# Memory attention's value product turned round, and the first block's expert lists made ready apart from their gates

## The chip, the cores and the metric

One core of a Trainium2 chip runs one program. TensorE (PE) multiplies, VectorE (DVE), ScalarE (ACT) and GpSimd (POOL) work on vectors, SyncE (SP) issues most transfers; ACT and POOL issue some too. The metric is the device time of one execution in microseconds (us), the median of several runs; lower is better.

## The reference

One decoder layer on 320 tokens: 256 of a prompt and 8 sequences of 8. Branches (convolution, DeltaNet, attention into a memory) are gated, summed and projected; then comes PEER, in which each token picks 128 single-neuron experts. The two parts that the change touches:

```python
def memory_attention(q, mem_k, mem_v):          # 4 heads of 256, 256 memory tokens; the 8 sequences have their own k and v
    s = jnp.einsum('blhd,bmhd->bhlm', q, mem_k).astype(jnp.float32) * (XA_HEAD_DIM ** -0.5)
    p = jax.nn.softmax(s, axis=-1)
    o = jnp.einsum('bhlm,bmhd->blhd', p, mem_v)

def block(xblk):                                 # peer_ffn, 8 heads, 16 experts each
    t1, i1 = lax.top_k(s1, PEER_TOPK)            # s1, s2: scores of a head's query halves against 128 keys each
    t2, i2 = lax.top_k(s2, PEER_TOPK)
    top, pos = lax.top_k(cand, PEER_TOPK)        # cand: the 16 x 16 sums t1 + t2; cidx: i1 * 128 + i2
    eidx = jnp.take_along_axis(cidx, pos, axis=-1)
    gate = jax.nn.softmax(top, axis=-1)
    u = expert_u[eidx]                           # 128 rows of 2048 floats (1 MB) for each token
    act = jax.nn.gelu(jnp.einsum('td,thkd->thk', xblk, u))
    v = expert_v[eidx]                           # another 1 MB
    return jnp.einsum('thk,thkd->td', gate * act, v)
```

## The kernel before

Everything is float32 and feature-major (128 features on the partitions, tokens in the free dimension), but for the hidden rows of the expert stage. SP streams 1 MB weight tiles into slots 0 to 5 of `ring`, a tile being issued when the one four (later five) before it has been used (`tiles_done`). The stages, one after the other: memory keys and values, convolution, 16 DeltaNet heads, four attention heads (`att`, 1190 to 1362 us), the merge of the branches for the first block of 128 tokens (`merge0`), its output projection (`out0`) and its queries for the experts (`pq0`, 1720 to 1785 us). From then on the expert stage runs over 320 tokens, and beside its first 128 tokens the same merge, projection, queries and picking are done for the other 192 tokens (`second_block(s)`, a step s behind each token).

**Attention.** For a head `a`, PE multiplies the scores of the prompt (L729, all 256 tokens) and of the 8 sequences (L737). L737 puts four column groups of 32 side by side: the masked queries of two sequences are stationary, a sequence's 128x256 keys move. Then it projects the queries of head `a + 1` (L522), while DVE and ACT do the softmax (L1641 to L1648, L1114), transposes the probabilities (L746, L747), and makes the values. Here the stationary operand is 128x128 of values: for the prompt 4 products with 256 moving columns (L758), for the sequences 32 products with 8 moving columns (L764), each recorded as two. Values come as tiles 4 and 5 of a head, freed when their half of L764 is done. DVE copies the result into `xoT0` and `xoT1` (L1658).

**First block, hidden rows.** After the first query tile of `pq0`, PE turns the normed hidden rows to token-major (L792). ACT and DVE split them into three bfloat16 parts, 512 columns at a time, in turn (L1136, L1697, L1140, L1701), ACT stores them to `hparts`, and SP waits for the store (`parts_out`) ahead of `token_parts` (L467) and of the loads of `merge1`.

**First block, picking.** For each of 8 heads `topk_part` runs on DVE: parts 0 and 1 take 16 of 128 twice, part 2 takes 16 of the 256 sums, part 3 turns positions into expert numbers (for each of the two key halves: compare L1764, multiply L1768, sum L1770; then L1772) and makes the head's gate by softmax (L1752, ACT's Exp L1154, L1775 to L1779). A head's scores need two query tiles. ACT takes its orders in one list: it copies a query (L1166), a score (L1160), and does a head's Exp in between.

**The lists.** PE runs three merge tiles of the second block and only then turns both lists, `efull` (numbers) and `gfull` (gates) (L835, L836). DVE copies them to `eT` and `gT` (L1786, L1787), clears two banks, and `lists_ready` at 2 lets POOL begin its gathers (L1953 for u, L1956 for v): four slots each, 1 MB a gather, a slot refilled when `dotted` or `summed` says that its token was used. DVE's dot (L1851) is two instructions of 1.22 us per token.

```python
            pool.wait_ge(lists_ready, 2)
            with pool.Fori(0, 8) as i:
                gather_pair(i)
```

Of the kernel before, what the change touches and what calls it, by code (L numbers as in the profile page):

```python
# [21 lines left out]
P = 128  # L22
D = 2048
# [101 lines left out]
def build(nc, io):  # L125
    with ExitStack() as ctx:
# [126 lines left out]
        xqs = (xq, seven[:, 4 * P:4 * P + 2 * TOKENS].rearrange("p (t n) -> p t n", t=2))  # L253
        mx, sm, r3 = sb("mx", [P, UNITS]), sb("sm", [P, UNITS]), sb("r3", [P, UNITS])
# [17 lines left out]
        def topk_buffers(flat, at, units):  # L272

            def piece(*shape, dt=F32, words=None):
                f = view(flat, at, int(np.prod(shape)) if words is None else words)
                if dt != F32:
# [6 lines left out]
                        cand2=piece(units, TOPK * TOPK), eq=piece(n, TOPK, dt=BF16, words=n * TOPK // 2),  # L283
                        v16=piece(2, units, TOPK), iu=piece(2, units, TOPK, dt=U32), i16=piece(2, units, TOPK, dt=BF16, words=n),
                        fdig=piece(2, n, dt=BF16, words=n), pos=piece(units, TOPK, dt=U32), digits=piece(2, n, dt=U32),
                        e12=piece(2, n), top=piece(units, TOPK), gx=piece(units, TOPK), gsum=piece(units, 1),
# [7 lines left out]
        hres0 = mmf[:, 0:1024].rearrange("p (n d) -> p n d", n=2)  # L294
# [27 lines left out]

        def softened(s):

            if s < LAST_TOPK:
                return [(s - TOPK_AT) // 4] if s >= TOPK_AT and (s - TOPK_AT) % 4 == 2 else []
            return {LAST_TOPK + 1: [6], LAST_TOPK + 4: [7]}.get(s, [])
# [183 lines left out]
        def _(pe):  # L511
# [211 lines left out]
            for a in range(AH):  # L723
# [122 lines left out]
            def turn_pair(n):  # L846
# [3 lines left out]
                for x in two:  # L850
                    if n:
                        pe.wait_ge(rest_ready, 8 + 4 * (n - 1) + x + 1)
                    turn_hidden(ps[6 + x], P if t == 1 else NS, t * P, q + x).then_inc(turned, 1)

            def query_tile(m):
                arrived("pq1", m % 4, m // 4)
                if m == 0:
                    pe.wait_ge(rest_ready, 8 + 12 + 1)
                project(regions[0], m % 4, h1_, free=((q_read[(m - 1) % 2], 8 + (m - 1) // 2 + 1),))

            def scores1(m):
                b = m % 2
                pe.wait_ge(q_read[b], 8 + m // 2 + 1)
                if m == 0:
                    pe.wait_ge(rest_ready, 8 + 12 + 2)
# [21 lines left out]
            def turn_lists():  # L887
                pe.wait_ge(picked, 2 * PH)
                pe.wait_ge(turned_read, 8)
                for n, name in enumerate(("efull", "gfull")):  # L890
                    for t in two:
                        w = P if t == 0 else NS
                        last = nc.tensor.transpose(ps[6 + n][:, t * P:t * P + w], tk1[name][0:w, t, :], ident[0:w, 0:w])
                last.then_inc(lists_turned, 1)
# [64 lines left out]
        def _(act):  # L959
# [150 lines left out]
            for a in range(AH):  # L1110
# [7 lines left out]
                act.wait_ge(pt_done, a + 1)  # L1118
                fn(pT[:, :, 0:TP], ps[6].rearrange("p (m t) -> p m t", m=2), ACT.Copy).then_inc(pt_ready, 1)
            with act.Fori(0, KT) as i:  # L1120
# [10 lines left out]
            def split_pair(n, t, q, w, banks):  # L1131
# [5 lines left out]
                hres = hres1 if t else hres0  # L1137
                for x in two:
                    act.wait_ge(rest_ready, 4 * n + x + 1)
                    fn(p[1][0:w, (q + x) * 512:(q + x + 1) * 512], hres[0:w, x, :], ACT.Copy).then_inc(part_taken, 1)  # L1140

            def store_parts(n, t):
                act.wait_ge(rest_ready, 4 * n + 4)
                act.wait_ge(part_taken, 4 * n + 4)
# [6 lines left out]
            def soften(n):  # L1151
                gx = (tk0 if n < PH else tk1)["gx"]
# [9 lines left out]
            for m in range(KT):  # L1162
# [4 lines left out]
                if m == 0:  # L1167
                    for n in two:
# [890 lines left out]
```

## Time and profile before

| | |
|---|---|
| median of 3 runs (lowest, highest) | 3784.81 us (3783.73, 3788.24) |
| the profiled execution | 3782.26 us |
| its span in the trace | 3780.2 us |
| mean granted clock of TensorE | 0.835 |
| busy: PE, DVE, ACT, POOL | 84%, 47%, 17%, 21% |
| gathers (software queue) | 671.13 MB, from 1822.56 us on |

The trace gives each instruction its start and its length; an engine's idle time is given with what ended it. The granted clock is a share of full speed (1.0 is 2.4 GHz, 0.5 is 1.2 GHz); a stretch's figure is a mean over it. Lengths of matmuls are modelled, starts are recorded.

### The profile page before, as it was taken

The page shows a single profiled execution, that of the slowest core. Times are in us where ns is not written, and L with a number is a line of the kernel's source. Part 1 is how long each engine was busy: PE and PEld are TensorE (multiplying, and loading weights), DVE is VectorE, ACT ScalarE, POOL GpSimd, SP SyncE. Part 2 cuts the span into 40 slices and gives each one's busy share as a digit, 9 for nine tenths or more (in the row PEclk, how much of TensorE's full clock was granted, in tenths as well). Part 3 has the DMA queues.
Part 4 walks back from the last instruction along what each step waited for, and adds up shares of the span by engine and source line. Part 5 has one row for each costly group of instructions (what it writes and reads, how often), then busy time and mean ns, then how long its engine had stood idle before and what let it go on. Part 6 is the DMA issues. An engine that isn't in the chain of part 4 may idle for free.

```text
span 3780.2 us, 50527 instructions
## 1 busy us (share of the span) xinstructions
PE 3168.2 (84%) x17796; PEld 2135.5 (56%) x17796; DVE 1791.1 (47%) x4287; ACT 628.5 (17%) x1657; POOL 777.1 (21%) x889
## 2 busy tenths in 40 slices
PE   8999999999997999998899999878665666665554
PEld 7767777777775789998788888645310000000000
DVE  2396656666564200006433333359955444444544
ACT  1001222222222100001011101122211111111111
POOL 1000111121111000000222222232233333333332
PEclk9999999999998889999999999978755555555555
DMA  5433334333332468886899999999999999999997
GB/s 189 147 120 137 129 107 132 118 120 119 115 96 91 172 225 294 292 290 237 334 419 417 419 417 418 418 406 417 356 397 418 416 418 418 416 418 414 415 416 301
DMA packets 203479, 1096.07 MB, mean 290 GB/s; under 512 B 27360, under 2 KB 69216, under 8 KB 75952
## 3 DMA queue, kind: packets, MB, share of 16 engines
q0 software_dynamic: 92160, 671.13, 43.2%
q1 hardware_dynamic: 104096, 401.31, 29.8%
q10 hardware_dynamic: 7120, 22.22, 1.5%
q8 instruction: 68, 1.11, 0.1%
q14 instruction: 35, 0.29, 0.0%
HBM read 1062.88 MB, written 31.70 MB: 290 GB/s over the span
## 4 chain that ended last, share of the span: by engine, by line
PE 43%; DMA 29%; DVE 17%; issue 8%; ACT 2%; POOL 2%; DVEq 0%; SPq 0%; ACTq 0%; POOLq 0%
PE psum L522 24%; DMA branches<-in_peer_u,idx 23%; PE psum L588 8%; DMA ring<-in_peer_u,idx 5%; DVE branches L1851 2%; PE psum L946 2%; DVE branches L1385 2%; DVE ring L1851 2%; DVE branches L1488 2%; PE psum L651 1%; PE psum L660 1%; PE psum L657 1%; PE psum L764 1%; PE psum L349 1%; DVE rs L1582 1%
## 5 line engine op out<-in xcount | busy, mean ns | idle before, releaser
L1851 DVE CUSTOM_DVE_ANT_0 ring<-ring,psum 128x1024 f32<-128x1024 f32 x480 | 566.7, 1219 | 638.3 <-DMA ring<-in_peer_u,idx 577.6
L522 PE MATMUL psum<-hT,ring 128*128 128x128 f32 (+2 forms) x4800 | 803.8, 328 | 29.2 <-DMA ring<-in_w_glu 10.5
L522 PEld LDWEIGHTS psum<-hT,ring 128*128 128x128 f32 x4800 | 720.7, 196 | 104.9 <-issue 31.8
L929 PE MATMUL psum<-shared,selb 24*128 24x512 bf16 x1280 | 304.8, 524 | 453.4 <-DVE dots L1851 443.9
L929 PEld LDWEIGHTS psum<-shared,selb 24*128 24x128 bf16 x1280 | 56.6, 96 | 1022.4 <-DVE dots L1851 921.7
L588 PE MATMUL psum<-hT,ring 128*128 128x320 f32 x2112 | 621.9, 436 | 9.9 <-DMA ring<-in_w_att 7.7
L588 PEld LDWEIGHTS psum<-hT,ring 128*128 128x128 f32 x2112 | 383.0, 191 | 152.8 <-issue 20.3
L1245 ACT ACTIVATE ge<-dots 128x1 f32<-128x1 f32 x320 | 94.3, 295 | 1485.9 <-DVE dots L1851 1480.3
L1851 DVE CUSTOM_DVE_ANT_0 branches<-branches,psum 128x1024 f32<-128x1024 f32 x160 | 189.0, 1218 | 238.9 <-DMA branches<-in_peer_u,idx 220.8
L522 PE MATMUL psum<-branches,ring 128*128 128x128 f32 (+1 forms) x2048 | 295.5, 303 | 6.3 <-ACT shared L1181 6.3
L522 PEld LDWEIGHTS psum<-branches,ring 128*128 128x128 f32 x2048 | 285.9, 192 | 10.0 <-issue 10.0
L1953 POOL DMA_INDIRECT ring<-in_peer_u,idx x240 | 225.9, 941 | 287.1 <-DVE dots L1851 249.9
L522 PE MATMUL psum<-mm,ring 128*128 128x128 f32 (+2 forms) x1504 | 250.5, 328 | 1.2 <-DVE mm L1677 1.2
L522 PEld LDWEIGHTS psum<-mm,ring 128*128 128x128 f32 x1504 | 232.9, 192 | 17.5 <-issue 5.0
L1665 DVE SCALAR_TENSOR_TENSOR shared<-shared,psum 128x128 f32<-128x128 f32 (+1 forms) x96 | 27.9, 318 | 361.8 <-PE psum L522 361.8
L1933 POOL TENSOR_TENSOR mm<-mm,shared 128x256 f32<-128x256 f32 (+1 forms) x112 | 100.9, 934 | 255.1 <-DVE mm L1520 255.1
L946 PE MATMUL psum<-branches,wz 128*8 128x512 f32 x640 | 126.9, 879 | 15.5 <-ACT wz L1247 10.2
L1385 DVE SCALAR_TENSOR_TENSOR branches<-branches,dwp 128x256 f32<-128x256 f32 x464 | 138.0, 378 | 0.0
L1944 POOL COPY idx<-shared 128x8 uint32 x40 | 7.8, 195 | 621.5 <-DVE shared L1787 621.3
L946 PE MATMUL psum<-vmem,wz 128*8 128x512 f32 x640 | 129.5, 895 | 5.5 <-ACT wz L1247 3.0
L1956 POOL DMA_INDIRECT vmem<-in_peer_v,idx x80 | 75.1, 939 | 270.9 <-PE psum L946 259.2
L946 PE MATMUL psum<-mm,wz 128*8 128x512 f32 x640 | 126.7, 878 | 2.1
(393 smaller groups left out, 3101.6 us busy)
## 6 DMA issues: line engine op xcount, KB each, us to landing
ring<-in_w_merge SPq DMA_DIRECT2D x160, 1024.0 KB
ring<-in_w_head SPq DMA_DIRECT2D x64, 1024.0 KB
ring<-in_w_outp SPq DMA_DIRECT2D x32, 1024.0 KB
ring<-in_w_pq SPq DMA_DIRECT2D x32, 1024.0 KB
ring<-in_w_att SPq DMA_DIRECT2D x24, 1024.0 KB, 7.0
ring<-in_w_mem SPq DMA_DIRECT2D x16, 1024.0 KB
ring<-in_w_glu SPq DMA_DIRECT2D x16, 1024.0 KB
out_qkv_out<-ring ACTq DMA_DIRECT2D x16, 520.5 KB
```

Of the source, the lines that this page charges most:

```text
L349: last = nc.tensor.matmul(out, ones[:], src[:, kt, :], start=kt == 0, stop=kt == count - 1)
L522: last = mat(out, ring[:, j, (k0 + kt) * P:(k0 + kt + 1) * P], src[:, kt, :], start=kt == 0, stop=kt == kts - 1)
L588: last = mat(ps[j][:, 0:TOKENS], ring[:, j, kt * P:(kt + 1) * P], hT[:, kt, :], start=kt == 0, stop=kt == KT - 1)
L929: last = mat(ps[q][:, :], selb[32 * q:32 * q + 24, j, :], hb[32 * q:32 * q + 24, g_, :], start=True, stop=True)
L946: last = mat(psum[32 * q:32 * q + group, 4 + g_, :], wz[:, g_, r % group, :], v_slots[s][:, q * 512:(q + 1) * 512], start=r % group == 0, ...
L1245: fn(ge[:, g_, j:j + 1], dots[:, g_, j, 0:1], ACT.Gelu_apprx_tanh, bias=dots[:, g_, j, 1:2]).then_inc(ge_ready, 1)
L1385: st(v.scalar_tensor_tensor(acc_, src, w, acc_, ALU.mult, ALU.add))
L1488: st(v.reciprocal(nrm[:, :, :], nrm[:, :, :]))
L1851: v.tensor_tensor_reduce(out=u, in0=u, in1=x, scale=1.0, scalar=0.0, op0=ALU.mult, op1=ALU.add, accum_out=dots[:, g_, j, half_:half_ + 1]) ...
L1933: g.tensor_tensor(lt[:, l, 0:units * P].rearrange("p (u n) -> p u n", u=units), at3[:, 0:units, :], lm[:, l, :].unsqueeze(1).to_broadcast( ...
L1953: g.indirect_dma_start(u_slots[s], None, io["peer_u"], at_).then_inc(u_in[s], 16)
L1956: g.indirect_dma_start(v_slots[s], None, io["peer_v"], at_).then_inc(v_in[s], 16)
```

## The change

The sequences' value product has the probabilities stationary, in four column groups, and the values moving: 16 products of 128x32 with 128x256, as L737 has. Its result is token-major; ACT copies it to `otok`, and two products with a selection of `ident` turn it back. The prompt's products stand between. The first block's hidden rows are copied whole to `hres0`, ACT makes the three parts at query tiles 0, 4 and 8, and POOL makes the two rests. In both blocks the two key halves are picked in one set of instructions of twice the size, and the softmax is done once for all eight heads, behind the picking. The first block's numbers are turned after two merge tiles (twice; the first copy goes nowhere), the gates after the third; the gathers wait for the numbers alone.

PE in the attention, and behind `pq0`:

```diff
-                pe.wait_ge(pt_ready, 2 * a + 2)
+                pe.wait_ge(pt_ready, 3 * a + 2)
...
+                for m in two:
+                    for c in two:
+                        for q in range(4):
+                            b = 2 * q + c
+                            at_ = (b % 4) * 512 + m * 256
+                            last = mat(ps[3][32 * q:32 * q + 32, 0:256], pz[:, m, c, 32 * q:32 * q + 32],
+                                       ring[:, 4 + b // 4, at_:at_ + 256], start=m + c == 0, stop=m + c == 2, skip_group_check=True)
+                            if m + c == 2 and q % 2:
+                                last.then_inc(tiles_done, 1)
...
-                for b in range(NBATCH):
-                    c = slice(TP + b * TS, TP + (b + 1) * TS)
-                    for d in two:
-                        for m in two:
-                            at_ = (b % 4) * 512 + m * 256 + d * P
-                            last = mat(ps[4 + d][:, c], ring[:, 4 + b // 4, at_:at_ + P], pT[:, m, c], start=m == 0, stop=m == 1)
-                    if b % 4 == 3:
-                        last.then_inc(tiles_done, 1)
+                pe.wait_ge(pt_ready, 3 * a + 3)
+                for d in two:
+                    last = mat(ps[4 + d][:, TP:TOKENS], otok[:, d * P:(d + 1) * P], tokens_of_slots, start=True, stop=True)
+                last.then_inc(pt_done, 1)
...
-            for k in range(3):
+            for k in range(2):
                 merge_tile(0, k)
             pe.wait_ge(picked, PH)
-            nc.tensor.transpose(ps[0][:, 0:P], tk0["efull"][:, 0, :], ident[:]).then_inc(summed, SLOTS)
+            nc.tensor.transpose(ps[2][:, 0:P], tk0["efull"][:, 0, :], ident[:]).then_inc(summed, SLOTS - 1)
+            nc.tensor.transpose(ps[0][:, 0:P], tk0["efull"][:, 0, :], ident[:]).then_inc(lists_turned, 1)
+            merge_tile(0, 2)
+            pe.wait_ge(picked, PH + 1)
             nc.tensor.transpose(ps[1][:, 0:P], tk0["gfull"][:, 0, :], ident[:]).then_inc(lists_turned, 1)
+            nc.tensor.transpose(ps[2][:, P:2 * P], tk0["gfull"][:, 0, :], ident[:]).then_inc(summed, 1)
```

ACT in the attention, then its first parts in `pq0` (called at query tiles 0, 4 and 8):

```diff
+                act.wait_ge(tiles_done, min(FIRST["att"] + 6 * a + 8, FIRST["att"] + 6 * AH))
+                fn(otok, ps[3][:, 0:256], ACT.Copy).then_inc(pt_ready, 1)
...
+            def first_parts(m):
+
+                act.wait_ge(rest_ready, m)
+                if m == 0:
+                    for q in range(4):
+                        act.wait_ge(turned, q + 1)
+                        last = fn(hres0[:, q * 512:(q + 1) * 512], ps[q], ACT.Copy)
+                    last.then_inc(part_taken, 1)
+                    act.wait_ge(part_taken, 1)
+                fn(parts[:, m, :], hres0, ACT.Copy).then_inc(part_taken, 1)
+                if m == 2:
+                    act.wait_ge(part_taken, 4)
+                    act.dma_start(hparts[0:P], parts[:, :, :]).then_inc(parts_out, 16)
...
-            soften(6)
-            soften(7)
-            for n in range(3):
-                gate(0, n)
+            gate(0, 0)
+            gate(0, 1)
+            soften(0)
+            gate(0, 2)
...
-                for n in softened(s):
-                    soften(PH + n)
+                if s == LISTS_AT:
+                    soften(1)
```

DVE: part 3 of `topk_part` compares, multiplies and sums both halves at once (the compare is shown), and the softmax is outside:

```diff
+                    st(v.tensor_tensor(eq, fdig.rearrange("p x n -> p (x n)").unsqueeze(2).to_broadcast([P, 2 * units * TOPK, TOPK]),
+                                       iota16[:].unsqueeze(1).to_broadcast([P, 2 * units * TOPK, TOPK]), ALU.is_equal))
...
+            def gates_in(tk, n):
+
+                units = tk["units"]
+                for t in range(units):
+                    top = tk["gfull"][:, t, :].rearrange("p (h k) -> p h k", h=PH)
+                    gx = tk["cand"][:, t, 0:PH * TOPK].rearrange("p (h k) -> p h k", h=PH)
+                    last = v.tensor_tensor(gx, top, top[:, :, 0:1].to_broadcast([P, PH, TOPK]), ALU.subtract)
+                last.then_inc(soft_in, 1)
...
+            def gates_out(tk, n):
+                units = tk["units"]
+                dve.wait_ge(soft_out, n + 1)
...
+            gates_in(tk0, 0)
+            v.memset(ps[5], 0.0).then_inc(dotted[1], SLOTS)
             dve.wait_ge(lists_turned, 1)
             v.tensor_copy(eT[:, 0:N0], ps[0][:, 0:N0]).then_inc(lists_ready, 1)
+            gates_out(tk0, 0)
+            st(v.memset(ps[4], 0.0))
+            dve.wait_ge(lists_turned, 2)
             v.tensor_copy(gT[:, 0:N0], ps[1][:, 0:N0]).then_inc(lists_ready, 1)
...
+                elif s == LISTS_AT:
+                    gates_out(tk1, 1)
```

POOL, ahead of its gathers:

```diff
+            for m in two:
+                pool.wait_ge(part_taken, m + 2)
+                if m:
+                    pool.wait_ge(rest_ready, m)
+                g.tensor_tensor(hres0, hres0, parts[:, m, :], ALU.subtract).then_inc(rest_ready, 1)
...
             pool.wait_ge(stored, 32)
-            pool.wait_ge(lists_ready, 2)
+            pool.wait_ge(lists_ready, 1)
```

`gates_out` waits for ACT's one Exp over all heads, then sums, inverts and multiplies (L1775 to L1779 of before, over 128 elements), and adds one to `picked`.

## Rows read from the trace of the kernel before

**Rows 1.** Page, the span in 40 slices: what the DMA engines moved

```profile
GB/s 189 147 120 137 129 107 132 118 120 119 115 96 91 172 225 294 292 290 237 334 419 417 419 417 418 418 406 417 356 397 418 416 418 418 416 418 414 415 416 301
```

**Rows 2.** Windows: stretch, its us, busy us by engine, granted clock, DMA share, GB/s

```profile
1247.00:1265.00 18.00, 17.65 (x113) 14.74 (x113) 1.42 (x9) 0.29 (x1) 0.00 (x0) 0.72 0.50 176
1344.00:1362.00 18.00, 16.84 (x72) 16.03 (x71) 1.02 (x4) 0.00 (x0) 0.00 (x0) 0.50 0.22 75
1785.00:1811.00 26.00, 12.86 (x66) 12.40 (x66) 24.32 (x115) 0.87 (x4) 0.00 (x0) 0.85 0.45 162
2700.00:2755.00 55.00, 28.15 (x132) 8.67 (x132) 51.43 (x172) 15.21 (x34) 14.78 (x17) 0.63 0.81 300
```

**Rows 3.** Groups by line, 1190 to 1362 us: busy us, mean ns, idle

```profile
L764 PE MATMUL psum<-ring 128*128 128x8 f32 x256 | 43.5, 314 | 0.0
...
L729 PE MATMUL psum<-kmem,ring 128*128 128x256 f32 x32 | 13.0, 579 | 0.0
...
L737 PE MATMUL psum<-ring 128*32 128x256 f32 x128 | 9.0, 430 | 0.0
```

**Rows 4.** Timeline of PE in the attention: start, us, what, count

```profile
1224.83 1.89 PE L729 MATMUL psum<-kmem,ring 128*128 128x256 f32 x8
...
1249.18 9.46 PE L764 MATMUL psum<-ring 128*128 128x8 f32 x64
...
1258.49 3.76 PE L729 MATMUL psum<-kmem,ring 128*128 128x256 f32 x8
...
1347.18 13.66 PE L764 MATMUL psum<-ring 128*128 128x8 f32 x64
```

**Rows 5.** The attention's tile loads, from issue to landing

```profile
DMA to landing us min/median/max: 4.9/7.0/7.5
```

**Rows 6.** Timeline of DVE, the first block's picking

```profile
1735.89 0.49 DVE L1720 MAX8 vmem<-vmem 128x8 f32<-128x128 f32 x2 [3.28 <-ACT vmem L1160]
...
1795.98 0.49 DVE L1720 MAX8 vmem<-vmem 128x8 f32<-128x128 f32 x2
...
1802.14 0.42 DVE L1764 TENSOR_TENSOR vmem<-vmem,iota 128x256 bf16<-128x256 bf16 x1
...
1804.62 0.18 DVE L1772 SCALAR_TENSOR_TENSOR vmem<-vmem 128x16 f32<-128x16 f32 x1
...
1805.32 0.49 DVE L1720 MAX8 vmem<-vmem 128x8 f32<-128x128 f32 x2
...
1820.02 0.29 DVE L1786 CAST shared<-psum 128x128 uint32<-128x128 f32 x1 [5.40 <-PE psum L836]
```

**Rows 7.** The chain that ended last, in order of time

```profile
1749.32 0.50 DVE vmem L1720 x2
```

**Rows 8.** Timeline of DVE, a head of the second block

```profile
2646.29 0.69 DVE L1764 TENSOR_TENSOR branches<-branches,iota 128x512 bf16<-128x512 bf16 x1
...
2648.22 0.75 DVE L1764 TENSOR_TENSOR branches<-branches,iota 128x512 bf16<-128x512 bf16 x1
```

**Rows 9.** Timeline of ACT during the first block's queries

```profile
1727.93 1.23 ACT L1140 ACTIVATE mm<-mm 128x512 bf16<-128x512 f32 x2 [0.27 <-DVE mm L1697]
...
1739.05 0.28 ACT L1166 ACTIVATE shared<-psum 128x128 f32<-128x128 f32 x1 [3.30 <-PE psum L522]
```

**Rows 10.** Timeline of PE: the third merge tile

```profile
1811.62 8.07 PE L522 MATMUL psum<-branches,ring 128*128 128x192 f32 x32 [6.34 <-ACT shared L1181]
```

**Rows 11.** Timeline of POOL: the first gather

```profile
1822.56 1.16 POOL L1953 DMA_INDIRECT ring<-in_peer_u,idx  x1 [1.53 <-DVE psum L1789]
```

**Rows 12.** Timeline of POOL in a DeltaNet head

```profile
734.53 6.31 POOL L1933 TENSOR_TENSOR mm<-mm,shared 128x384 f32<-128x384 f32 x7 [14.47 <-DVE mm L1520]
```

**Rows 13.** Timeline of DVE in the same head

```profile
733.30 0.56 DVE L1516 TENSOR_TENSOR ring<-ring 128x384 f32<-128x384 f32 x1
...
734.83 1.11 DVE L1522 TENSOR_TENSOR ring<-ring,shared 128x384 f32<-128x384 f32 x1
```

**Rows 14.** Timeline of SP's queue

```profile
1770.15 3.48 SPq L467 DMA_DIRECT2D shared<-hparts  x8
```

More of the change, by code:

```diff
@@ L253, in build @@
         xqs = (xq, seven[:, 4 * P:4 * P + 2 * TOKENS].rearrange("p (t n) -> p t n", t=2))
+        at = [4 * P + 2 * TOKENS]
+        pz = view(seven, at, 4 * P).rearrange("p (m c n) -> p m c n", m=2, c=2)
+        otok = view(seven, at, 2 * P)
+        tokens_of_slots = ident[:].rearrange("p (q n) -> p q n", q=4)[:, :, 0:2 * TS]
         mx, sm, r3 = sb("mx", [P, UNITS]), sb("sm", [P, UNITS]), sb("r3", [P, UNITS])
@@ L893, in turn_lists @@
                         last = nc.tensor.transpose(ps[6 + n][:, t * P:t * P + w], tk1[name][0:w, t, :], ident[0:w, 0:w])
[L894 removed]
+                    last.then_inc(lists_turned, 1)
             def second_block(s):
@@ L1166, in _ @@
                 fn(qs[:, b, 0:N0], ps[4 + b][:, 0:N0], ACT.Copy).then_inc(q_read[b], 1)
-                if m == 0:
-                    for n in two:
-                        split_pair(n, 0, 2 * n, N0, (2 * n, 2 * n + 1))
-                    store_parts(1, 0)
-                else:
+                if m:
                     take_scores0(m - 1)
-                if m >= 5 and m % 2:
-                    soften((m - 5) // 2)
+                if m in (0, 4, 8):
+                    first_parts(m // 4)
             take_scores0(KT - 1)
@@ L1648, in _ @@
                 v.tensor_tensor(pp, pp, sm[:].unsqueeze(2).to_broadcast([P, UNITS, MEM]), ALU.mult).then_inc(pn_ready, 1)
-                dve.wait_ge(pt_done, a + 1)
+                dve.wait_ge(pt_done, 2 * a + 1)
                 for m in two:
-                    last = v.tensor_copy(pT[:, m, TP:].rearrange("p (q n) -> p q n", q=4),
-                                         ps[7][:, m * P:(m + 1) * P].rearrange("p (q n) -> p q n", q=4)[:, :, 0:2 * TS])
+                    for c in two:
+                        at_ = slice(c * TS, (c + 1) * TS)
+                        last = v.tensor_copy(pz[:, m, c, :].rearrange("p (q n) -> p q n", q=4)[:, :, at_],
+                                             ps[7][:, m * P:(m + 1) * P].rearrange("p (q n) -> p q n", q=4)[:, :, at_])
                 last.then_inc(pt_ready, 1)
@@ L1710, in topk_part @@
                 combos = [(x, t) for x in two for t in range(units)]
-                v16, iu, sc2, cand, cand2, top, pos, gx = (tk[n] for n in ("v16", "iu", "sc2", "cand", "cand2", "top", "pos", "gx"))
+                at_ = slice(h * TOPK, (h + 1) * TOPK)
+                v16, iu, sc2, cand, cand2, pos = (tk[n] for n in ("v16", "iu", "sc2", "cand", "cand2", "pos"))
+                top = tk["gfull"][:, :, at_]
                 def lst(x, t):
@@ L1780, in topk_part @@
-                    dve.wait_ge(picked, first + h + 1)
+                    st(v.tensor_reduce(e12.rearrange("p x n -> p (x n)"), eq, AX, ALU.add))
+                    st.wait()
+                    v.scalar_tensor_tensor(tk["efull"][:, :, at_], e12[:, 0, :].rearrange("p (t k) -> p t k", t=units),
+                                           float(NK), e12[:, 1, :].rearrange("p (t k) -> p t k", t=units), ALU.mult, ALU.add)\
+                        .then_inc(picked, 1)
+            def gates_in(tk, n):
[5 more added lines that the diff above has]
+                last.then_inc(soft_in, 1)
@@ new lines, in gates_out @@
+            def gates_out(tk, n):
+                units = tk["units"]
+                dve.wait_ge(soft_out, n + 1)
+                for t in range(units):
+                    gx = tk["cand"][:, t, 0:PH * TOPK].rearrange("p (h k) -> p h k", h=PH)
+                    st(v.tensor_reduce(tk["gsum"][:, t * PH:(t + 1) * PH, 0], gx, AX, ALU.add))
+                st.wait()
+                st(v.reciprocal(tk["gsum"], tk["gsum"]))
+                st.wait()
+                for t in range(units):
+                    gx = tk["cand"][:, t, 0:PH * TOPK].rearrange("p (h k) -> p h k", h=PH)
+                    last = v.tensor_tensor(tk["gfull"][:, t, :].rearrange("p (h k) -> p h k", h=PH), gx,
+                                           tk["gsum"][:, t * PH:(t + 1) * PH, :].to_broadcast([P, PH, TOPK]), ALU.mult)
+                last.then_inc(picked, 1)
```

84 lines of the change are left out of this document (32 added, 52 removed).

## The prediction

> **What bounds the kernel.** I went through the page's slices first. From the slice that begins at 1890 us to the end the DMA engines move 414 to 419 GB/s in nearly every slice [rows 1], whichever work lies beside, so from the first gather on the kernel is bound by transfers: the 671 MB of gathers and the weights of the second block. One has 406; two fall clearly short, 356 and 397 GB/s, at 2646 to 2835 us. Before the first gather no engine binds all along: PE does where weights stream, and where PE waits the transfers idle too (162 GB/s at 1785 to 1811 us [rows 2]), since ring slots come free only as PE uses them. Hence two rules for this change. Time taken off the chain ahead of the first gather, which is issued at 1822.56 us [rows 11], moves the whole rest forward. Time taken off DVE, ACT or PE behind it is worth something only where the transfers lag, 2700 to 2755 us above all: 300 GB/s with DVE busy for 51.43 of 55 us [rows 2].
>
> **The attention.** Its windows are filled by PE, so its products are on the chain. L764's 32 small products for each of 4 heads (256 records) are busy for 43.5 us [rows 3]. What replaces them has L737's shape to the letter (128x32 stationary, 256 moving, four column groups, 16 products a head), and L737 took 9.0 us for four heads, its slower passes included [rows 3]. The two products that turn the result back have 64 moving columns, four records a head. I have no row of that shape; L764's 9.46 / 64 = 0.15 us a record is the lower bound and L729's 1.89 / 8 = 0.24 us (256 columns) the upper [rows 4], so 0.6 to 0.95 us a head; near the lower end, 2.6 us for four. Result: 43.5 - 9.0 - 2.6 = 31.9 us.
>
> Then the clock. L729, the next head's scores, takes 1.89 us ahead of the first L764 and 3.76 us right behind it [rows 4]; the window of L764 and what follows has a granted clock of 0.72, a mixture of the two levels, and the last head's has 0.50, 1.2 GHz all through [rows 2]. L764 feeds 8 columns a product, and the clock falls while it runs. If the denser products keep it at 2.4 GHz, L729's 13.0 us [rows 3] become 4 x 1.89 = 7.6, another 5.4 us. The last head follows a pause for its softmax, so I leave that one at 1.2 GHz: 9.0 / 4 = 2.25 us becomes some 3.9, minus 1.6. Hidden: ACT's copy of `otok` runs under L758, which was moved between the two; the four DVE copies in place of two run under ACT's longer copy; clearing `pz` runs while DVE would wait for ACT's squares. New risk: V tiles are given back early in the head, and the tiles of the query after next are issued only then. They are needed L758 (1.99 us), the turning back, L729 and L737 later, about 7 us at full clock, and a tile takes 4.9 / 7.0 / 7.5 us to land [rows 5]. I charge 1 us in all. Sum: 31.9 + 5.4 - 1.6 - 1 = 34.7, say 35 us. Bounds: without any gain of clock 29, with the last head at full clock and no stall 40.
>
> **From the queries to the first gather.** DVE is the chain here. A head of picking takes 1805.32 - 1795.98 = 9.34 us, and the first takes 1749.32 - 1735.89 = 13.43 [rows 6, 7]: it stood 4.1 us for its Exp, which comes late in ACT's list and behind a table load. Picking thus ended at 1735.89 + 13.43 + 7 x 9.34 = 1814.7 us. In the new form:
> - The two passes over the key halves (1802.14 to 1804.62, 2.48 us [rows 6]) become one of twice the size. The second block runs this very size now, one pass from 2646.29 to 2648.22, 1.93 us [rows 8]. Saved: 0.55.
> - The softmax goes: 1804.62 to 1805.32 [rows 6] without L1772's own share (about 0.1) is 0.6, and L1752 about 0.1.
> - So a head takes 9.34 - 1.25 = 8.1 us. Its scores come each 7.6 us (two query tiles at 3.8), so DVE remains the chain, narrowly. Eight heads from 1735.89 end at 1800.7.
> - The eight rest operations that DVE did before 1732 us go; nothing moves forward by it, since the first head waits for the second query tile's scores at 1735.9.
> - ACT: two copies of 512 columns take 1.23 us [rows 9], so a copy of 2048 takes at most 2.5 us. ACT is idle for 3.30 us in each 3.8 us of a query tile [rows 9], so the parts fit.
> - POOL: seven operations of 256 to 384 elements (2176 together) take 6.31 us [rows 12], so one of 2048 takes up to 6 us. The first is mostly over when DVE begins, the second falls into DVE's second head. DVE operations with two inputs in SBUF are slowed by such a neighbour: L1522 takes 1.11 us with POOL at work from 734.53, L1516 of the same size 0.56 just before [rows 12, 13]. One blocked operation costs between nothing and 6 us; I take 2.2, between the ends, because only three of a head's operations are of that kind.
>
> The Trainium skill (SBUF — State Buffer, Who interferes with whom) states this as an exclusive lock: a DVE instruction with two SBUF inputs and a GpSimd one that reads SBUF take turns for whole instructions. The row of L1522 agrees (0.55 us longer, less than one POOL operation); by the rule a long POOL operation is the worst neighbour, and the sum would have up to 6 us in place of 2.2.
>
> Picking then ends at 1802.9. Before, 7.9 us passed from there to the first gather (1814.7 to 1822.56), since PE had merge tile three, 8.07 us from 1811.62 [rows 10], ahead of the transposes, and DVE two copies and two clearings ahead of POOL's start (copy at 1820.02 [rows 6]). Now PE has only two tiles ahead and stands ready. DVE does one subtraction and one clearing (0.7 us, the transposes beside it), copies the numbers, and POOL follows 1822.56 - 1820.02 = 2.5 us behind as now, less the gate copy and clearings: 1.8. First gather: 1802.9 + 0.7 + 1.8 = 1805.4, 17.2 us sooner. The gates come behind: Exp, three small operations, merge tile three, their transposes, a copy. That holds back the first dot, not the gathers; eight are under way, 8.4 MB or 20 us of transfers, and the fourth v gather's slot is given back long before POOL comes to it.
>
> Given back: the ring holds about one tile less when the gathers begin (two merge tiles used, not three), so 1.05 MB more must move behind that point, 2.5 us at 418 GB/s. Net: 14.7, say 15 us. Bounds 9 (6 us for the lock, 2 more for a thin first backlog) and 20.
>
> The store of the parts goes out some 28 us later, about 1760. SP needed it at 1770.15 [rows 14], and 1.6 MB take a few us. Cover: about 6 us there, then ring tiles worth some 10 us.
>
> **Beside the expert stage.** A head of the second block loses about 0.65 + 0.6 + 0.1 = 1.35 us of DVE time (a pass of 1.93 us twice [rows 8] becomes one of about 3.2). With query tiles beside it, transfers are at their limit and nothing comes of it. Some 2.5 heads lie where they lag: 3.4 us, and 1 to 2 us earlier. Against it at `LISTS_AT`: one late Exp with its table load, for which DVE stands about 2.4 us, and about 1.8 us of gate operations. Net 1 us gained; bounds 6 gained (the stretch recovers more, because ACT loads its table once rather than eight times) and 3 lost.
>
> **Sum.** 35 + 15 + 1 = 51 us off the profiled execution's 3782.26: 3731. The median stands 2.5 us above that execution, so 3784.81 - 51 = 3734.
>
> **Rivals.**
> - The clock stays at 1.2 GHz in the attention. For it: in this very place it fell each time before [rows 2, 4]. Against: L737 ran just ahead of query stretches at full clock. L764's substitute would take 4 x 3.9, turning 5, L729 15 in place of 13: 43.5 - 15.6 - 5 - 2 = 21 gained. Total 37, 3748. Chance 0.1.
> - Transfers no longer bind the start of the expert stage: PE's first dot comes forward by less than the gathers, and then the stage goes at PE's pace, 32 us for four tokens against 32.6 by transfers. For it: these two are close. Against: the slices stand at 418 [rows 1]. The lead of 15 would shrink to about 5: 3744. Chance 0.1.
> - The DVE-bound stretch gives more: 300 GB/s for 55 us leaves 15 us on the table [rows 2]. If two thirds come back: 3724. Chance 0.1.
> - The change does nothing for the end, because the stage is bound by the same megabytes whenever it starts. Against: its bytes are the same, but its start moves. Chance under 0.01.
> - Slower: the store of the parts lands late, and SP, which waits for it ahead of the merge tiles and of the rows for the first dot, holds the stage. Each us beyond about 1781 then costs one, and it decides from 1781 + 51 = 1832 us on, that is with POOL's two operations at some 30 us each rather than 6. At 60 us late: about 3794. Chance 0.02.
> - Lesser mishaps that keep a gain of 10 to 30 us (store late by 20 us, DVE blocked repeatedly): about 3760, 0.04.
>
> The forecast has the rest, 0.63, its own range 3722 to 3745. The range 3718 to 3750 leaves out the slow cases and the far end of the third: 2 in 10. A change within 0.2% (7.6 us), which is about what this kernel's measurement cannot tell from none: 0.01. Faster: 0.97. Slower: 0.02.
>
> **What would show it.** The value products near 2.3 us a head and L729 near 1.9; merge of the first block beginning near 1327; heads of picking 8.1 us apart without the gap behind the first, but for one operation in the second that stands beside POOL; the first gather near 1770 on the new time axis (1822.6 - 35 - 17); 418 GB/s from there; a DVE wait of some 2 us for the one late Exp. It would be wrong if L729 stayed at 3.8, if SP stood in front of `token_parts`, or if the slices behind the first gather fell below 410 GB/s.

## The result

| | before | after |
|---|---|---|
| median (lowest, highest) | 3785.27 us (3783.73, 3788.24) | 3727.03 us (3721.23, 3729.36) |
| the profiled execution | 3782.26 us | 3729.36 us |
| its span | 3780.2 us | 3727.5 us |
| first gather | 1822.56 us | 1769.58 us |

The ratio is 0.9845 [0.9821, 0.9868]: 58 us less by the medians, 53 us by the two profiled executions. The forecast was 3734 us.

The page of the kernel after, what the DMA engines moved in 40 slices of the span:

```profile
GB/s 192 142 126 141 116 122 120 121 118 119 120 114 83 179 287 293 294 287 234 413 417 418 417 419 418 411 408 417 364 414 416 418 418 415 416 416 415 413 416 295
```

Of the two short slices of before, 356 and 397 GB/s [rows 1], one is left, at 364. The expert stage still runs at the transfers' pace, and it begins one slice earlier.

**The attention.** Groups by line on PE, 1195 to 1327 us. L756 is the new value product, L768 the turning back, and L727, L735 and L765 are L729, L737 and L758 of before:

```profile
L756 PE MATMUL psum<-ring 128*32 128x256 f32 x128 | 9.4, 445 | 2.7 <-ACT ring L1126 2.7
L765 PE MATMUL psum<-ring,vmem 128*128 128x256 f32 x32 | 8.2, 398 | 0.0
L735 PE MATMUL psum<-ring 128*32 128x256 f32 x128 | 7.7, 382 | 0.0
L727 PE MATMUL psum<-kmem,ring 128*128 128x256 f32 x32 | 7.7, 384 | 0.0
...
L768 PE MATMUL psum<-ident,ring 128*128 128x64 f32 x16 | 2.2, 261 | 0.0
```

The timeline of PE around the first and the last head's values:

```profile
1251.94 1.93 PE L756 MATMUL psum<-ring 128*32 128x256 f32 x32 [0.69 <-ACT ring L1126]
1253.81 1.99 PE L765 MATMUL psum<-ring,vmem 128*128 128x256 f32 x8
1255.64 0.55 PE L768 MATMUL psum<-ident,ring 128*128 128x64 f32 x4
1256.03 1.95 PE L727 MATMUL psum<-kmem,ring 128*128 128x256 f32 x8
...
1319.48 3.64 PE L756 MATMUL psum<-ring 128*32 128x256 f32 x32 [0.69 <-ACT ring L1126]
1323.05 2.20 PE L765 MATMUL psum<-ring,vmem 128*128 128x256 f32 x8
...
1327.23 7.41 PE L520 MATMUL psum<-hT,ring 128*128 128x128 f32 x64 [1.60 <-DVE branches L1680]
```

A head's values and their turning back take 1.93 + 0.55 us where L764 took 9.46, and the next head's scores take 1.95 us where they took 3.76 [rows 4]: the clock no longer falls. The windows say the same (columns as in [rows 2]): 1.00 in the value stretch of the first head, where 1247 to 1265 us had 0.72, and 1.00 at the start of the merge.

```profile
1251.90:1257.90 6.00, 5.96 (x52) 4.34 (x52) 1.24 (x7) 0.38 (x1) 0.00 (x0) 1.00 0.90 325
1327.00:1345.00 18.00, 17.77 (x159) 17.77 (x160) 0.78 (x3) 0.83 (x3) 0.00 (x0) 1.00 0.77 275
```

In the last head the transposes and L756 (3.64 us) run at 1.2 GHz, behind the 4.09 us for which PE stands for the softmax: 1317 to 1323 us have a granted clock of 0.50. L765 behind them is back at 2.20. The groups of before that the other passes are compared with, and PE's first merge tiles there, which took 9.34 us where the new ones take 7.41:

```profile
L758 PE MATMUL psum<-ring,vmem 128*128 128x256 f32 x32 | 9.8, 458 | 2.7 <-ACT ring L1119 2.7
...
1362.34 9.34 PE L522 MATMUL psum<-hT,ring 128*128 128x128 f32 x64 [1.50 <-DVE branches L1659]
```

**The picking.** The timeline of DVE in the first block. L1739 begins a head, L1753 makes the 256 sums, and L1780, L1785 and L1787 are the joined compare, multiply and sum:

```profile
1699.24 0.49 DVE L1739 MAX8 vmem<-vmem 128x8 f32<-128x128 f32 x2 [16.34 <-ACT vmem L1182]
...
1701.99 0.41 DVE L1753 TENSOR_TENSOR vmem<-vmem 128x256 f32<-128x256 f32 x1
...
1705.40 0.69 DVE L1780 TENSOR_TENSOR vmem<-vmem,iota 128x512 bf16<-128x512 bf16 x1
...
1707.40 0.48 DVE L1739 MAX8 vmem<-vmem 128x8 f32<-128x128 f32 x2
...
1710.14 2.80 DVE L1753 TENSOR_TENSOR vmem<-vmem 128x256 f32<-128x256 f32 x1
...
1717.94 0.48 DVE L1739 MAX8 vmem<-vmem 128x8 f32<-128x128 f32 x2
...
1766.74 0.17 DVE L1789 SCALAR_TENSOR_TENSOR vmem<-vmem 128x16 f32<-128x16 f32 x1
...
1767.76 0.29 DVE L1823 CAST shared<-psum 128x128 uint32<-128x128 f32 x1
...
1786.68 1.21 DVE L1894 CUSTOM_DVE_ANT_0 ring<-ring,psum 128x1024 f32<-128x1024 f32 x1
```

Heads begin 8.15 us apart, but for the second, which takes 10.54. In it L1753 takes 2.80 us where it took 0.41 in the first, and ends (1712.94) within 0.3 us of POOL's second subtraction (1712.67):

```profile
1708.58 4.09 POOL L1989 TENSOR_TENSOR mm<-mm 128x2048 f32<-128x2048 f32 x1 [10.42 <-ACT mm L1159]
...
1769.58 1.16 POOL L2002 DMA_INDIRECT ring<-in_peer_u,idx  x1 [1.00 <-POOL idx L1993]
```

The first gather is issued 2.84 us behind the last pick (L1789); before, it took 7.9 us. SP's queue loads the parts at 1733.50 us and the merge tiles right behind, so the later store holds nobody:

```profile
1733.50 3.48 SPq L465 DMA_DIRECT2D shared<-hparts  x8
1737.02 23.17 SPq L373 DMA_DIRECT2D ring<-in_w_merge  x7
```

**Where the 53 us are.** Read off the two traces, stage by stage:

| stretch | before | after | gained |
|---|---|---|---|
| start to the first head's scores (L729 / L727) | 1224.83 | 1229.42 | -4.6 |
| first scores to the first merge tile | 137.5 | 97.8 | 39.7 |
| first merge tile to the first expert score | 368.9 | 367.4 | 1.5 |
| first expert score to first gather | 91.3 | 75.0 | 16.3 |
| first gather to the end | 1957.6 | 1957.9 | -0.3 |

(The first expert score is the first product of a query with the keys, 1731.26 and 1694.61 us.) The first row lies ahead of all that the change does to PE's work. In 1190 to 1200 us the last DeltaNet head had a granted clock of 1.00 in the profiled execution of before and 0.69 in that of after. The other eleven traces have their first scores between 1222 and 1230 us, so this is the spread of single executions, and it accounts for 4.6 of the 5.3 us by which the two profiled ones differ less than the medians. The last row hides two things that cancel, which the experiments below take apart.

### The profile page after: what moved, and what is told of

It is laid out like the page before. It is cut to its first block, busy times and chain, and to the rows that moved or that the text cites. A ratio compares the mean times of both kernels' runs of the same rounds, so it can differ in the third digit from the quotient of the medians.

```text
span 3727.5 us, 50183 instructions
## 1 busy us (share of the span) xinstructions
PE 3126.9 (84%) x17686; PEld 2090.6 (56%) x17686; DVE 1775.4 (48%) x4187; ACT 613.4 (16%) x1632; POOL 789.8 (21%) x891
## 4 chain that ended last, share of the span: by engine, by line
PE 43%; DMA 29%; DVE 16%; issue 8%; ACT 2%; POOL 1%; DVEq 0%; SPq 0%; ACTq 0%; POOLq 0%
PE psum L520 25%; DMA branches<-in_peer_u,idx 24%; PE psum L586 8%; DMA ring<-in_peer_u,idx 4%; DVE branches L1894 2%; PE psum L953 2%; DVE branches L1403 2%; DVE branches L1506 2%; DVE ring L1894 1%; PE psum L649 1%; PE psum L658 1%; PE psum L655 1%; PE psum L347 1%; DVE rs L1600 1%; POOL ring L1982 1%
## 5 line engine op out<-in xcount | busy, mean ns | idle before, releaser
L953 PE MATMUL psum<-kmem,wz 128*8 128x512 f32 x640 | 126.9, 879 | 2.5 <-ACT wz L1265 0.3
```

The lines of the kernel that those rows point to most:

```text
L953: last = mat(psum[32 * q:32 * q + group, 4 + g_, :], wz[:, g_, r % group, :], v_slots[s][:, q * 512:(q + 1) * 512], start=r % group == 0, ...
```

## The experiments

The kernels of one group ran on one chip, beside before. Times by trace are counted from the first expert score of the same trace, since what lies ahead of it spreads by some us: in before the first gather comes at 91.3 us, the first dot at 103.7, the 65th u gather at 600.5 and the end at 2048.9; in after 75.0, 92.1, 587.0 and 2032.9. Two more traces of after end at 2030.4 and 2030.7, so a difference of the ends below some 3 us says nothing.

### One half of the change alone

att_only is before with the attention's hunks alone, rest_only is before with all the others.

> Only the attention's value product is changed; everything behind it is as before. My theory (each us saved ahead of the first gather moves the end): the trace after showed 39.7 us less between the first scores and the first merge tile, and 2 us more behind it by the clock, so 40 to 42 us faster, about 3744. Rival (the two parts hinge on each other, the stage behind takes some of it back): under 35 us faster. If the clock gained nothing, L727's form would be at 3.8 us behind the values instead of 1.95.

> Everything but the attention's product. My theory: first gather 15.8 us sooner, 3 us of it given back, 3 us won beside the expert stage: 14 to 17 us faster, about 3770. Together with the attention alone this must give the whole 58. Rival (the picking's gain depends on the attention): clearly under 12 or over 20.

| | median | ratio | first attention score to first expert score | first gather | first dot | end |
|---|---|---|---|---|---|---|
| before | 3784.64 | | 506.4 | 91.3 | 103.7 | 2048.9 |
| att_only | 3740.28 | 0.9885 [0.9868, 0.9901] | 464.9 | 91.6 | 102.4 | 2051.3 |
| rest_only | 3760.80 | 0.9939 [0.9923, 0.9956] | 503.3 | 74.9 | 91.8 | 2029.4 |

The attention gives 44 us by the medians and 41.5 by its own trace, against a forecast of 35 in the sum. The rest gives 24 by the medians, more than expected; by its trace it is 16.4 up to the first gather and 3.1 behind it. Another 3.1 lie in its attention, whose code is that of before: the granted clock in 1250 to 1300 us was 0.85 there and 0.78 in before, so they are spread and no gain. By their own stretches the halves add up: 41.5 + 19.5 = 61, where the medians of after in the three groups lie 58 to 64 us below their before. The medians of the halves themselves add up to 68, each known to some 6 us, so they don't contradict it. Neither half needs the other.

### What the start of the expert stage hangs on

gather_late holds the first gather back on POOL, dot_late the first dot on DVE; everything else is the change's.

```diff
             pool.wait_ge(lists_ready, 1)
+            for _ in range(34):
+                st(g.memset(hs_pool[:], 0.0))
+                st.wait()
```

```diff
             merge_cx(0)
             merge_d(0)
+            st(v.memset(mean[:], 1.0))
+            for _ in range(5):
+                st.wait()
+                st(v.reciprocal(mean[:], mean[:]))
+            st.wait()
```

> The whole change, and POOL stands for about 10 us (34 small memsets of a free tile) between the first list and its first gather; PE and DVE are free to go on. My theory (transfers bind everything from the first gather on): the end comes 9 to 10 us later than with the change, about 3737. Rival (PE's pace from the first dot binds, the gathers have 17 us of lead over the first dot): 0 to 4 us later.

> The whole change, and DVE stands for about 11 us (five reciprocals of a free tile) ahead of its first dot; the gathers start as before. My theory (transfers bind; 8 gathers and the ring's tiles are under way, some 25 to 30 us of transfers): the end comes 0 to 5 us later than with the change. Rival (PE's and DVE's pace binds): about 11 us later.

| | median | ratio | first gather | first dot | 65th u gather | end |
|---|---|---|---|---|---|---|
| after (profiled) | 3727.03 | 0.9845 | 75.0 | 92.1 | 587.0 | 2032.9 |
| gather_late | 3729.20 | 0.9852 [0.9836, 0.9868] | 81.0 | 92.1 | 592.0 | 2035.5 |
| dot_late | 3730.33 | 0.9857 [0.9841, 0.9874] | 74.9 | 103.5 | 597.9 | 2040.6 |

The added clearings turned out shorter than planned: the gather came 6.0 us later, not 10. Of these 6.0 us 5.0 were still there at the 65th gather, and 2.6 to 5.1 at the end. The dot came 11.4 us later, the 65th gather 10.9, and the end 7.7 to 10.2. The other traces of after have the 65th gather at 587.0 and 586.6, so there the shifts are far beyond the spread; by the medians alone neither kernel can be told from after, since the intervals overlap. The transfers don't cover the late dot, and this is my expectation's miss: I had the backlog of eight gathers hide all but 0 to 5 us of it, and the rival, about 11, came nearer. The windows show where the transfers run dry. dot_late, 26 us behind its first gather and on (its columns as before):

```profile
1792.44:1798.44 6.00, 1.62 (x6) 0.69 (x6) 5.93 (x9) 1.00 (x1) 0.30 (x1) 0.50 0.66 274
1798.44:1804.44 6.00, 6.00 (x28) 6.00 (x28) 1.21 (x4) 1.47 (x5) 0.64 (x1) 0.72 0.51 178
1804.44:1810.44 6.00, 6.00 (x42) 4.69 (x41) 2.37 (x4) 0.92 (x3) 1.88 (x2) 1.00 0.69 244
1810.44:1816.44 6.00, 6.00 (x42) 4.69 (x41) 2.37 (x4) 0.91 (x3) 1.87 (x2) 1.00 0.91 343
```

And the change itself in the same stretch:

```profile
1795.58:1801.58 6.00, 6.00 (x44) 5.34 (x44) 2.37 (x4) 0.59 (x2) 1.88 (x2) 1.00 1.01 419
1801.58:1807.58 6.00, 6.00 (x42) 4.92 (x42) 2.37 (x4) 0.92 (x3) 1.88 (x2) 1.00 1.02 422
1807.58:1813.58 6.00, 6.00 (x42) 4.69 (x41) 3.35 (x7) 0.59 (x2) 1.88 (x2) 1.00 1.02 423
1813.58:1819.58 6.00, 6.00 (x39) 6.00 (x38) 0.00 (x0) 0.33 (x1) 0.00 (x0) 1.00 1.00 415
```

Taking 419 GB/s as full, dot_late's transfers lack the equivalent of 9.9 us between 2 and 62 us behind its first gather, those of the change 1.1 and those of before 0.9. So both ends of the loop are near the limit at its start: a gather 6.0 us later costs 5.0, and of a dot 11.4 us later 0.5 us (by the 65th gather) to 2.6 us (by the transfers, 11.4 less 8.8) are covered. Part of that price is the clock's: PE stood while DVE did, and the granted clock behind was 0.50 and 0.72. The ninth and tenth u gathers are 10.2 us apart there where they are 8.1 with the change, so some 2 us of the 10.9 are this, and the room is an estimate, 0.5 to 3 us.

dot_late is also the kernel in which only the gathers come forward: its first gather is at 74.9, as with the change, and its first dot at 103.5, where before has 103.7. Against before its 65th gather comes 2.6 us sooner and its end 8.3; the change's come 13.5 and 16.0 to 18.5 us sooner. So without the 11.6 us by which the first dot moved, most of the gain at the 65th gather and about half of it at the end would be missing (the end holds what is won beside the expert stage as well). Before, the dot came 12.4 us behind the first gather; now it comes 17.1 behind, which leaves it 4.7 us less room than it had.

### Single suspects

The next group makes one edit each in the kernel after. tile3 runs the third merge tile ahead of both turnings, in the 7.2 us for which PE stands there; pool_split cuts POOL's subtraction of 2048 columns into eight of 256; exp_early gives ACT the second block's gate Exp one step sooner, as the last order of that step, so that DVE doesn't stand for it.

```diff
-            for k in range(2):
+            for k in range(3):
                 merge_tile(0, k)
             pe.wait_ge(picked, PH)
...
-            merge_tile(0, 2)
             pe.wait_ge(picked, PH + 1)
```

```diff
-                g.tensor_tensor(hres0, hres0, parts[:, m, :], ALU.subtract).then_inc(rest_ready, 1)
+                for c in range(0, D, 256):
+                    last = g.tensor_tensor(hres0[:, c:c + 256], hres0[:, c:c + 256], parts[:, m, c:c + 256], ALU.subtract)
+                last.then_inc(rest_ready, 1)
```

```diff
-                if s == LISTS_AT:
-                    soften(1)
                 if s - 1 in TURN_X2:
                     take_tokens(TURN_X2[s - 1])
+                if s == LISTS_AT - 1:
+                    soften(1)
```

> The changed kernel unchanged, as the measure for the three kernels of the same call: 3721 to 3730 us.

> The whole change, but the third merge tile is again ahead of the lists' transposes. PE stood idle for 7.2 us there in the trace after, and the tile takes 5.4. My theory: first gather at the same time (within 0.5 us), first dot about 6 us sooner, one ring tile more loaded ahead of the gathers, so the 3 us that the lead fell by become about 0.5: 2 to 3 us faster than the change. Rival (the fall of the lead is a ramp of the gathers, and the tile has no part in it): no change within 1 us. If the tile holds up the transposes after all: up to 2 us slower.

> The whole change, with each of POOL's two subtractions cut into eight of 256 elements. My theory (a DVE operation with two inputs in SBUF waits for the whole POOL operation beside it): the one DVE operation of 2.80 us in the second head of picking falls to 1 us or less, perhaps a few others gain 0.3; first gather 1.5 to 2 us sooner, end the same amount. Rival (2.8 us is the price of the neighbour's total work, however cut): the second head takes as long as before, 10.5 us.

> The whole change, with the second block's one Exp asked of ACT a step sooner, right behind the last head of picking. My theory (DVE's 2.4 us stand for the Exp lies where transfers lag): the stand is gone, and the lead over the kernel before at gather 140 is 2 us larger; 1 to 2 us faster at the end. Rival (the lag is made up behind it anyway, because the transfers had nothing to wait for): no change at the end. Risk: ACT waits for DVE in that step, and PE's transposes behind it come later.

| | median | ratio | first gather | first dot | 65th u gather | end |
|---|---|---|---|---|---|---|
| after_again | 3722.14 | 0.9837 [0.9822, 0.9851] | 74.9 | 92.1 | 587.0 | 2030.4 |
| tile3 | 3719.13 | 0.9825 [0.9812, 0.9839] | 74.8 | 88.7 | 584.3 | 2027.9 |
| pool_split | 3720.32 | 0.9832 [0.9819, 0.9846] | 73.2 | 91.2 | 585.3 | 2030.5 |
| exp_early | 3720.99 | 0.9832 [0.9817, 0.9847] | 74.9 | 92.1 | 586.8 | 2029.4 |

The intervals of all four overlap, so no median here tells one kernel from another, and what follows is read from the traces.

tile3: from the first gather to the 65th it takes 509.5 us, before 509.2, the change 512.0. PE waits for the numbers only 1.99 us in place of 7.22. The edit does two things: one more ring tile is used up when the gathers begin, and the first dot comes 3.4 us sooner. The bytes tell them apart. From the first gather to the 65th the change moves 212.9 MB and tile3 212.0, and 0.9 MB are 2.2 us at 418 GB/s; an earlier dot by itself takes no bytes away. So nearly all of the 2.5 us is the ring tile. before moved 212.5 MB and had 371 GB/s in its first 10 us where the change had 297, which fits a tile that was under way when the gathers began.

pool_split: the second head falls from 10.54 to 8.80 us, since L1753 takes 0.66 us with POOL's eight short pieces beside it:

```profile
1706.55 0.66 DVE L1753 TENSOR_TENSOR vmem<-vmem 128x256 f32<-128x256 f32 x1
1707.24 0.53 DVE L1757 CAST vmem<-vmem 128x32 bf16<-128x32 uint32 x1
```

The first gather comes 1.8 us sooner and the 65th 1.3 to 1.7, but the end no sooner than in the other traces. What became of the 1.5 us isn't shown; it is within what the ends spread by.

exp_early: the stand of DVE is gone. The timeline of DVE in after, then in exp_early:

```profile
2692.47 0.08 DVE L1894 DVE_READ_ACCUMULATOR2_ANT dots<- 128x1 f32 x1
2694.97 0.48 DVE L1807 TENSOR_REDUCE branches<-branches 128x8 f32<-128x128 f32 x2 [2.42 <-ACT branches L1176]
```

```profile
2687.02 0.08 DVE L1894 DVE_READ_ACCUMULATOR2_ANT dots<- 128x1 f32 x1
2687.02 0.47 DVE L1807 TENSOR_REDUCE branches<-branches 128x8 f32<-128x128 f32 x2
```

From the 127th u gather to the 141st it takes 65.1 us where the traces of after take 66.2 to 67.3 (before took 65.2), but neither the end nor the median can be told from those of after.

### The three together, and the key halves apart again

all_three has the three edits. two_passes is after with part 3 in two passes over the key halves, as before; the rest of the change stands.

```diff
-                    st(v.tensor_tensor(eq, fdig.rearrange("p x n -> p (x n)").unsqueeze(2).to_broadcast([P, 2 * units * TOPK, TOPK]),
-                                       iota16[:].unsqueeze(1).to_broadcast([P, 2 * units * TOPK, TOPK]), ALU.is_equal))
...
+                    for x in two:
+                        eqx = eq[:, x * n_:(x + 1) * n_, :]
+                        st(v.tensor_tensor(eqx, fdig[:, x, :].unsqueeze(2).to_broadcast([P, n_, TOPK]),
+                                           iota16[:].unsqueeze(1).to_broadcast([P, n_, TOPK]), ALU.is_equal))
...
```

> The changed kernel unchanged, as the measure of this call: 3719 to 3730 us.

> Third merge tile ahead of the lists, POOL's subtractions in eight pieces each, and the second block's Exp asked for a step sooner. My theory (each acts at its own place): counted from the first score product, first gather 1.8 us sooner than with the change, first dot 5 us sooner, end 3.5 (tile) + 1.5 (pieces) + 1.5 (Exp) = 6 to 7 us sooner; median 5 to 8 us under the changed kernel of the same call. Rival (they buy the same time, transfers that were idle once): 3 to 4 us.

> The whole change, but the two key halves are compared, multiplied and summed in two passes again, in both blocks; the softmax stays behind the picking. My theory: 0.55 us more for each of eight heads, first gather and first dot 4.4 us later, end 4 to 5 us later than with the change; beside the expert stage 0.65 us a head more, of which about 1.5 us shows. Rival (the picking waits for PE's scores in part, which come every 7.6 us): 0 to 2 us later.

| | median | ratio | first gather | first dot | 65th u gather | end |
|---|---|---|---|---|---|---|
| after_third | 3720.61 | 0.9832 [0.9819, 0.9845] | 74.9 | 92.0 | 586.6 | 2030.7 |
| all_three | 3718.68 | 0.9831 [0.9817, 0.9844] | 73.0 | 84.8 | 581.7 | 2025.7 |
| two_passes | 3728.97 | 0.9853 [0.9839, 0.9866] | 79.1 | 95.8 | 591.6 | 2038.5 |

By its trace all_three is 5 us better than after; by the medians it is 2 us, and the intervals lie over each other, so a better kernel than after isn't shown. two_passes costs 7.8 us by the traces and 8.4 by the medians. Heads of the first block are 8.72 us apart in place of 8.15, which puts the first gather 4.2 us later: 7 times 0.57 is 4.0, and the second head takes 10.53 in both, since L1753 begins 2.1 us behind POOL's subtraction there in place of 1.6 and ends 0.28 us behind its end in both (2.22 us in place of 2.80). Another 3 us come beside the expert stage (587.7 us from the 65th to the 161st u gather against 584.8), where the second block's heads do the same with twice the elements.

## Why the prediction came out

The forecast of 3734 us was 7 above the median, inside its range. The mechanisms held; the size is closer than its parts, since some misses point opposite ways. Step by step, in the prediction's own terms:

**The value products: right, the surroundings undersized.** 43.5 - 9.0 - 2.6 was to be 31.9; it is 43.5 - 9.4 - 2.2 = 31.9, to the tenth by luck, since both terms were off by 0.4. The clock was put at 5.4 for L729; it is 13.0 - 7.7 = 5.3. What I left out is that the same clock serves the other passes too: L737 falls from 9.0 to 7.7 (1.3 us), L758 from 9.8 to 8.2 (1.6), and the stretch from the first merge tile on, which used to begin at 1.2 GHz, is 1.5 us shorter. What I charged for the last head (1.6) was right as to its product (3.64 us), but I had counted slow passes twice: L737's 9.0, which I took as the price, holds some already, and the 9.4 holds the last head's. Against it the last head's transposes became slower: L744 and L745 take 6.0 us where L746 and L747 took 5.2. The 1 us for late tiles did not occur: no row of the attention shows PE waiting for a load. Together 31.9 + 5.3 + 1.3 + 1.6 + 1.5 - 0.8 = 40.8, say 41 us in place of 35, with att_only's 41.5 beside it, just past the upper bound of 40. The term that was mis-sized is the clock's: it was sized by one line where a list of all lines in the slowed stretch was at hand.

**To the first gather: 16.3 for 17.2.** Heads of 8.15 us for 8.1; the lock 2.39 for 2.2; last pick to first gather 2.84 for 2.5 (0.7 + 1.8). The first head's wait of 4.1 us is gone. The Trainium skill (SBUF — State Buffer, Who interferes with whom) has a DVE instruction with two SBUF inputs and a GpSimd one that reads SBUF contend for a lock that one of them holds for its whole instruction. The traces agree: the sum of 256 elements lasted 2.80 us, in all nine traces with whole subtractions it ended 0.28 us behind POOL's, and in pool_split, with pieces of about 0.65 us, it lasted 0.66. The worst case of up to 6 us did not come, because DVE reached its first such operation 1.6 us after POOL's 4.09 us had begun, and POOL's operation was itself shorter than the bound from [rows 12]. That the first gather stands at 1769.58 where I had named 1770 is partly luck: the attention gave some 5 us more than I said, and the execution reached it 4.6 us late.

**Given back: 2.5 us for 2.5** (512.0 against tile3's 509.5, of which 2.2 by the bytes).

**Beside the expert stage: 3 to 5 us in place of 1.** From the 65th to the 161st u gather the traces of after take 584.3 to 586.0 us, before 589.3, rest_only 582.9 and two_passes 587.7. The joined halves are worth about 3 of it. The gain lies where I had put it: the lead over before grows by 2 us up to the 113th u gather and by 3.2 to 3.5 more up to the 125th, in the stretch in which DVE is busy nearly all along. That stretch moved 300 GB/s before [rows 2] and now moves 339, 5 us of transfers:

```profile
2646.00:2700.00 54.00, 28.20 (x138) 8.81 (x142) 49.72 (x160) 12.61 (x31) 16.10 (x17) 0.64 0.88 339
```

What I oversized is the charge against it, 4.2 us for the late Exp and the gate operations. The wait for the one Exp was right (2.42 us for 2.4), but exp_early, which is without it, is only 1 to 2 us faster there. The last row of the table in the result, 1957.6 against 1957.9, is the two cancelling: 2.5 to 2.9 us given back, 3.3 to 5.0 regained, and what is left over lies within the spread of single executions (1955.5 and 1955.8 in the two other traces of after).

**The rivals.** That the clock stays low is out: the windows of after have 1.00. The store held nobody: SP's queue goes from the query tiles straight to its parts at 1733.50. The six slices behind the first gather stand at 413 to 419 GB/s, so the start of the stage didn't go at PE's pace. But the rival named something real: dot_late shows that the first dot is on the path too, with no more than 0.5 to 3 us of room. With only the gathers forward, 2.6 of the 13.5 us were left at the 65th gather and 8.3 of 16 or more at the end. The prediction had called the gates something that holds back the first dot, "not the gathers"; how near the dot was to holding up the stage it did not see. (One later slice reads 408 GB/s; before had one of 406 there.) Of the third rival, that two thirds of the 15 us in the stretch bound by DVE come back, about a third did: 339 GB/s for 300.

By measured terms the sum is 41 + 16.3 - 2.7 + 4 = 58.6 us, as the medians have it (58.2). The same kernel lies 62 and 64 us under before in the other groups, so its value is known to some 5 us, and the agreement to 0.4 is luck.

**Left open.** Why the granted clock in the last DeltaNet head was 0.69 in one execution and 1.00 in another of the same code isn't shown; of the thirteen traces five have 1.00 there and eight 0.51 to 0.72. Nor was it tried whether the last head's pause could be filled, so that L756 runs at 2.4 GHz there too.

## What to carry over

Cost a product by what it streams: a head's values of the eight sequences took 9.46 us as stationary operands with 8 columns moving, and 1.93 us moving past 32-column probabilities in four groups, and behind the sparse form the next passes ran at 1.2 GHz, so sum over every line in the stretch whose clock it sets. When one resource binds a stage, find out how long the work queued at its start covers it before you call a later consumer free: here eight gathers left the first dot no more than 0.5 to 3 us of room, and bringing the gathers forward without it would have kept only part of the gain. A vector operation that reads two operands from SBUF can be held until the GpSimd operation beside it ends (0.41 us became 2.80), so charge up to the length of that one; cutting it into eight took the wait away and cost POOL about 1 us, off the chain here.

## What the hardware showed

- One GpSimd subtraction of 128x2048 f32 took 4.09 us, 2.0 ns a column, and held a DVE operation of 0.41 us for 2.39 us more; eight pieces of 256 took 5.06 to 5.25 us and held it for 0.25 us.
- The clock fell to 1.2 GHz while PE, by its rows, was busy without a gap on products of 8 columns [rows 4], and stayed at 2.4 GHz over products of 256 columns with the same values.
- A turning-back product with 64 moving columns took 0.14 us a record (0.55 / 4), near the 0.15 of one with 8 [rows 4].
- Transfers moved 415 to 423 GB/s in each 6 us of a stretch of 24, with PE busy all through.
- Behind eight gathers of 1 MB issued in a row, a first use 17.1 us after the first gather left the transfers 1.1 us short of 419 GB/s between 2 and 62 us behind it, a first use 28.6 us after it 9.9 us.
